# Gating mix with tokens on partitions, in products of 512 columns, turned back by DMA

## The chip, the core and the metric

The kernel runs on one core of one Trainium2 chip. The metric is the device time of one execution in microseconds: 1327.77 us before, the median of 3 runs (1327.48 to 1327.86). The engines are named as in the profile: PE is TensorE (PEld its weight load), DVE is VectorE, ACT is ScalarE, POOL is GpSimd, SP is SyncE, which here issues nearly all DMAs.

## What is computed

Two layers of a trunk. In each, one projection of the normalised input feeds four branches (A gated position mixing, B pooling, C latent attention, D stick-breaking attention), which are gated, summed and projected back. The change touches branch A only:

```python
def spatial_gating(u, v, ln_g, ln_b, w_s, b_s):
    b, s, _ = v.shape
    v = layer_norm(v, ln_g, ln_b)
    nb = s // SGU_BLOCK                                        # 4 blocks of 128 tokens
    vb = v.reshape(b, nb, SGU_BLOCK, SGU_GROUPS, SGU_GROUP_DIM)  # 4 groups of 128 channels
    pos_chunk = jnp.arange(SGU_BLOCK) // CHUNK
    mask = pos_chunk[None, :] <= pos_chunk[:, None]
    w = jnp.where(mask[None], w_s, jnp.zeros_like(w_s))
    mixed = jnp.einsum('gts,bnsgc->bntgc', w, vb) + b_s.T[None, None, :, :, None]
    return u * mixed.reshape(b, s, SGU_WIDTH)
```

Sequence 512, model width 1024, gating width 512.

## The kernel before

Every engine runs a program written out by hand, with semaphores between them. Values are float32; a product is made of three, since each operand is split into a high and a low part (`mm3`, lines 597 to 599: high x high, high x low, low x high). 128x128 blocks of weights are the stationary operand and up to 512 columns of activations the moving one, or the other way round.

**The weights** come in chunks of 8 blocks, in the order of `ORDER` (`chunk_order`), through a ring of four slots. For a chunk, SP loads `w_raw` once the chunk four before it is done (L464), ACT writes the rounded high part `w_hi` (L1037, where `weights_up_to` stands in ACT's program), and POOL subtracts to get `w_lo` (two instructions, L570 and L572). PE waits for `w_lo` before it starts the chunk.

**The stretch around the change**, in PE's order: the projection `bz2`; `mix`; the projection `bz3`; `kq0` (keys, then queries, of heads 0 and 1 into banks 0 to 3); then the first `pair_c` (p = 0): gates `gb0` to `gb3`, products of branch B `yb0`, `yb1`, the scores of two heads, `cz0`, `cz1`, the attention output of head 0 ("att0"), then the second `pair_c` (p = 1), which begins with `kq1`, the output of head 1 ("att1") and `gb4`.

- On PE, `mix` has for each of 4 groups and 4 token blocks one `mm3` of 128 columns: stationary the normalised values (`vn_hi`, `vn_lo`), moving the mixing weights. The result has channels on partitions, which is how it is needed. Then `pe.wait_ge(off_made)` and `bz3`.
- On ACT, `bz(2, 6)` (L1176) waits for the end of `bz2`, and `weights_up_to(l, "kq0")` behind it makes `w_hi` of `bz3`.
- On DVE, `front` makes `mix_off` (per channel and position: the bias and the norm's shift), then `gate_z(2)`, `gate_p(2)`, `b_low(2)`, `rope_tables()`, and then the four instructions of L1735, which take the four banks out of PSUM, scale by channel and add `mix_off` into `mix_t`. They release `mix_taken`, for which PE waits before the queries of `kq0`. `keys_summed` comes next.
- `mix_t` is read late, by `heads_d` (L1950).
- In `pair_c` on ACT, L1298 (`weights_up_to(l, kq, 7)`) is followed by the exponentials of head 0, which wait for the scores' maxima on DVE.
- In `pair_c` on DVE, near the end: `merge_p(0)`, `keys_low(n, 0)`, `gate_c(n, 6)`, `merge_p(1)`, `gate_c(n + 1, 7)`, `keys_low(n + 1, 1)`, `out_gated(n, 6)`, `out_low(n)`. `merge_p` (L1786) joins the two-byte halves of probabilities that a DMA has turned. ACT's `keys_high(n + 1, 1)` (L1239) waits for the second `merge_p(1)` copy; behind it on ACT stand `w_hi` of `gb4`, `keys_squared(l, 1)` with a load of a function table, and `out_high(n)`; DVE's `out_low(n)` follows, and PE's `gb4` waits for that (`act_c_made`).
- Turning by DMA is in use already for keys, queries and probabilities: ACT copies a float32 tile into two planes of two-byte halves (L1256, L1233), SP issues a `DMA_TRANSPOSE` (L471, L485), and DVE or ACT joins the halves again (L1861, L1786).

Of the kernel before, what the change touches and what calls it, by code (L numbers as in the profile page):

```python
# [7 lines left out]
F32 = mybir.dt.float32  # L8
# [8 lines left out]
P = 128  # L17
# [3 lines left out]
G = 4  # L21
# [108 lines left out]
def build(nc, x_in, p_in, pos_in, w_in, par_in, rows_in, const_in, out):  # L130
    ctx = ExitStack()
    with ctx:
# [40 lines left out]
        def plan(start, stop, *items):  # L173
# [22 lines left out]
        vn_hi, vn_lo, rows, mix_off, ln_t = plan(  # L196
            36, 58, ("vn_hi", [TB, SEQ], F32R), ("vn_lo", [TB, SEQ], F32R), ("rows", [SEQ], F32),
            ("mix_off", [G, P], F32), ("ln_t", [P], F32))
# [17 lines left out]
        (mix_t,) = plan(16, 24, ("mix_t", [G, SEQ], F32))  # L216
        k_tok, k_rot, q_tok = plan(36, 46, ("k_tok", [PAIR, TB, P], F32), ("k_rot", [TB, PAIR, 2, HALF], F32),
# [19 lines left out]
        (k_swap,) = plan(13, 14, ("k_swap", [TB, 2, HALF], F32))  # L237
# [35 lines left out]
        def sems(names):  # L273
# [18 lines left out]
        lat_squared, lat_var, lat_root, lat_scaled, lat_taken, lat_halved, lat_hi_made, lat_made = sems(  # L292
            "lat_squared lat_var lat_root lat_scaled lat_taken lat_halved lat_hi_made lat_made")
# [5 lines left out]
        mix_ready, mix_taken, krr_made = sems("mix_ready mix_taken krr_made")  # L299
# [157 lines left out]
        def _(sync):  # L457
# [22 lines left out]

            def turn_p(n, h):
# [35 lines left out]
            for l in range(DEPTH):  # L517
                for name in ORDER:
# [11 lines left out]
                    if name == "bx2":  # L530
                        turn_lat(l)
                    if name in TURNS_C:
                        p, h = TURNS_C[name]
                        turn_p(l * G + PAIR * p + h, h)
# [53 lines left out]
        def _(pe):  # L588
# [108 lines left out]
            def front(l):  # L697
# [45 lines left out]
                for g in range(G):  # L743
                    if g < 2:
                        pe.wait_ge(pooled, after(l * G + 3 - g))
                    for t in range(TB):
                        last = mm3(ps[:, g * 512 + t * P:g * 512 + (t + 1) * P], vn_hi[:, t, g * P:(g + 1) * P],
                                   vn_lo[:, t, g * P:(g + 1) * P], w_hi[:, g, :], w_lo[:, g, :])
# [279 lines left out]
        def _(act):  # L1028
# [222 lines left out]
            def pair_c(l, p):  # L1251
# [46 lines left out]
                weights_up_to(l, kq, 7)  # L1298
                exponentials(n, 0)
# [177 lines left out]
        def _(dve):  # L1477
# [80 lines left out]
            def front(l):  # L1558
# [161 lines left out]
                for g in range(G):  # L1720
                    c = slice(g * P, (g + 1) * P)
                    last = dve.scalar_tensor_tensor(mix_off[:, g, :], bank(5)[:, c], sm("ln_col", G + g), rows[:, c],
# [6 lines left out]
                rope_tables()  # L1729
                for g in range(G):  # L1730
                    if g < G - 1:
                        dve.wait_ge(mix_ready, after(l * (G - 1) + g))
                    else:
                        dve.wait_ge(*end_of(l, "mix"))
                    dve.scalar_tensor_tensor(mix_t[:, g, :].rearrange("p (t s) -> p t s", t=TB),  # L1735
                                             bank(g).rearrange("p (t s) -> p t s", t=TB), sm("ln_col", g),
                                             over(mix_off[:, g, :], [P, TB, P], 1), ALU.mult, ALU.add).then_inc(
# [435 lines left out]
```

## Time and profile before

| | |
|---|---|
| median of 3 runs | 1327.77 us |
| profiled execution | 1328.13 us, its span 1326.3 us |
| PE busy | 1319.2 us, 99% of the span |
| PEld, DVE, ACT, POOL busy | 83%, 58%, 49%, 47% |
| granted TensorE clock | 1.00 throughout |
| chain that ended last | PE 93%, DVE 4% |
| DMA engines' mean share | 38.6% for the busiest queue |

The span runs from the first to the last instruction; 1.8 us of the profiled execution lie around it. A matmul's duration in the trace covers its pipeline; what it costs in a stream is the distance between two starts. In a timeline the columns are start, duration, engine, line, operation, operands and count, then in brackets the idle time of the engine before it and what ended it.

### The profile page before, as it was taken

How to read it: one execution, taken by the hardware profiler on the slowest of the kernel's cores; microseconds unless marked ns; L12 is line 12 of the kernel's file. 1: busy time of each engine (PE TensorE's matmuls, PEld its weight loads, DVE VectorE, ACT ScalarE, POOL GpSimd, SP SyncE). 2: the span in 40 equal slices, each digit the busy share in tenths (PEclk: the TensorE clock that was granted, in tenths of full speed). 3: DMA queues.
4: the chain of work that ended last, by engine and by line, in shares of the span. 5: the costliest groups of instructions: out<-in, count | busy, mean ns of one | idle time of the engine just before them, and what ended most of it. 6: DMA issues, size and time to landing. Idle time of an engine off the chain costs nothing.

```text
span 1326.3 us, 15805 instructions
## 1 busy us (share of the span) xinstructions
PE 1319.2 (99%) x6103; PEld 1106.0 (83%) x6103; DVE 767.8 (58%) x1133; ACT 651.4 (49%) x979; POOL 621.3 (47%) x455
## 2 busy tenths in 40 slices
PE   9999999999999999999999999999999999999998
PEld 8778888888888888888888888888888888888887
DVE  7998676166663223274779976662666533333743
ACT  6478686266652222224455586754666422222242
POOL 2445353454444444455464543444444544444552
PEclk9999999999999999999999999999999999999999
DMA  7425554343343322323344264452433433333332
GB/s 213 117 78 127 128 148 105 94 115 99 100 115 96 95 95 96 112 95 96 97 119 119 87 143 106 125 123 92 107 108 103 112 95 96 96 97 117 101 97 95
DMA packets 141930, 144.63 MB, mean 109 GB/s; under 512 B 82704, under 2 KB 111648, under 8 KB 141856
## 3 DMA queue, kind: packets, MB, share of 16 engines
q1 hardware_dynamic: 140624, 143.08, 38.6%
q8 instruction: 48, 0.79, 0.3%
q10 hardware_dynamic: 1232, 0.55, 0.2%
q14 instruction: 26, 0.21, 0.1%
HBM read 123.15 MB, written 2.10 MB: 94 GB/s over the span
## 4 chain that ended last, share of the span: by engine, by line
PE 93%; DVE 4%; SPq 1%; ACT 1%; DMA 0%; issue 0%; ACTq 0%
PE ps L597 31%; PE ps L599 31%; PE ps L598 31%; SPq L464 1%; PE ps L784 1%; DVE n_t L1605 0%; DVE h_lo L1487 0%; DVE trail_a L1637 0%; DVE pool_lo L1487 0%; DVE trail_b L1637 0%; DVE xb L1640 0%; DVE vn_lo L1487 0%; DVE r_b L1595 0%; DMA par<-par_in 0%; DMA w_raw<-w_in 0%
## 5 line engine op out<-in xcount | busy, mean ns | idle before, releaser
L570 POOL TENSOR_TENSOR w_lo<-w_raw,w_hi 128x512 fp32r<-128x512 f32 x222 | 312.4, 1407 | 680.3 <-ACT w_hi L1037 680.0
L597 PE MATMUL ps<-h_hi,w_hi 128*128 128x512 f32 x1152 | 449.3, 390 | 1.8 <-DVE h_lo L1487 1.8
L599 PE MATMUL ps<-h_hi,w_lo 128*128 128x512 f32 x1152 | 448.4, 389 | 0.0
L598 PE MATMUL ps<-h_lo,w_hi 128*128 128x512 f32 x1152 | 448.4, 389 | 0.0
L1037 ACT ACTIVATE w_hi<-w_raw 128x1024 fp32r<-128x1024 f32 x227 | 238.4, 1051 | 160.6 <-PE ps L599 154.9
L572 POOL TENSOR_TENSOR w_lo<-w_raw,w_hi 128x512 fp32r<-128x512 f32 x222 | 312.0, 1405 | 0.0
L597 PEld LDWEIGHTS ps<-h_hi,w_hi 128*128 128x128 f32 x1152 | 216.2, 188 | 48.1 <-DVE h_lo L1487 3.4
L599 PEld LDWEIGHTS ps<-h_hi,w_lo 128*128 128x128 f32 x1152 | 216.2, 188 | 45.2
L598 PEld LDWEIGHTS ps<-h_lo,w_hi 128*128 128x128 f32 x1152 | 216.3, 188 | 44.3
L1976 DVE SCALAR_TENSOR_TENSOR m_part<-th,ps 128x512 f32<-128x512 f32 x48 | 33.0, 688 | 237.8 <-PE ps L599 237.7
L1336 ACT ACTIVATE th<-ps 128x512 f32<-128x512 f32 x48 | 28.7, 597 | 182.0 <-PE ps L599 182.0
L597 PE MATMUL ps<-act_hi,w_hi 128*128 128x512 f32 x192 | 74.8, 390 | 0.0
L598 PE MATMUL ps<-act_lo,w_hi 128*128 128x512 f32 x192 | 74.7, 389 | 0.0
L599 PE MATMUL ps<-act_hi,w_lo 128*128 128x512 f32 x192 | 74.7, 389 | 0.0
L597 PE MATMUL ps<-m_hi,w_hi 128*128 128x512 f32 x128 | 49.8, 389 | 0.0
L598 PE MATMUL ps<-m_lo,w_hi 128*128 128x512 f32 x128 | 49.8, 389 | 0.0
L599 PE MATMUL ps<-m_hi,w_lo 128*128 128x512 f32 x128 | 49.8, 389 | 0.0
L599 PEld LDWEIGHTS ps<-act_hi,w_lo 128*128 128x128 f32 x192 | 36.0, 188 | 7.5
L598 PEld LDWEIGHTS ps<-act_lo,w_hi 128*128 128x128 f32 x192 | 36.0, 188 | 7.4
L597 PEld LDWEIGHTS ps<-act_hi,w_hi 128*128 128x128 f32 x192 | 36.0, 188 | 7.4
L1427 ACT ACTIVATE o_sq<-x 128x512 f32<-128x512 f32 x16 | 10.1, 634 | 63.8 <-DVE x L2005 63.8
L597 PE MATMUL ps<-w_hi,act_hi 128*128 128x512 f32 (+1 forms) x96 | 36.9, 384 | 0.0
(341 smaller groups left out, 2098.7 us busy)
## 6 DMA issues: line engine op xcount, KB each, us to landing
w_raw<-w_in SPq DMA_DIRECT2D x180, 512.0 KB, 3.5
w_raw<-w_in SPq DMA_DIRECT2D x92, 128.0 KB, 2.5
w_raw<-w_in SPq DMA_DIRECT2D x36, 256.0 KB, 3.1
x<-x_in SPq DMA_DIRECT2D x8, 256.0 KB, 4.6
w_raw<-w_in SPq DMA_DIRECT2D x32, 64.0 KB, 2.1
out_x<-x SPq DMA_DIRECT2D x7, 256.0 KB, 4.0
p_raw<-p_in SPq DMA_DIRECT2D x2, 512.0 KB, 4.6
w_raw<-w_in ACTq DMA_DIRECT2D x4, 128.0 KB, 3.0
```

What stands on the lines that cost most here:

```text
L464: sync.dma_start(to, part).then_inc(raw_loaded[c % RING], 16)
L570: pool.tensor_tensor(w_lo_t[s][:, 0:4, :], w_raw_t[s][:, 0:4, :], w_hi_t[s][:, 0:4, :].bitcast(F32), ALU.subtract)
L572: pool.tensor_tensor(w_lo_t[s][:, 4:8, :], w_raw_t[s][:, 4:8, :], w_hi_t[s][:, 4:8, :].bitcast(F32), ALU.subtract).then_inc(w_lo_made, 1)
L597: pe.matmul(o, a_hi, b_hi, start=first, stop=False, skip_group_check=skip)
L598: pe.matmul(o, a_hi, b_lo, start=False, stop=False, skip_group_check=skip)
L599: return pe.matmul(o, a_lo, b_hi, start=False, stop=last, skip_group_check=skip)
L784: last = pe.matmul(ps[:, s:s + keys], q[at_, b * P:keys], k[at_, 0:keys], start=False, stop=q is qr_lo, skip_group_check=True)
L1037: act.activation(w_hi_t[s][:, 0:n, :], w_raw_t[s][:, 0:n, :], ACT.Copy).then_inc(w_hi_made, 1)
L1336: act.activation(th[:, i % 4, :], bank(b), ACT.Tanh, scale=0.5).then_inc(g_tanh, 1)
L1427: act.activation(o_sq[:, d % 2, :], tile(x, d), ACT.Square).then_inc(o_squared, 1)
L1976: dve.scalar_tensor_tensor(o, th[:, i % 4, :], 1.0, bank(b), ALU.add, ALU.mult).then_inc(y_taken, 1)
```

## The change

The mixing weights become stationary and the normalised values moving: one `mm3` for each group, 512 columns (four runs of 128 that stand 512 apart), so 12 products in place of 48 in each layer. The result has tokens on partitions. DVE copies the four banks as they are into `mix_tok`, now ahead of `rope_tables()`. In `pair_c` with p = 0, ACT splits each group into two-byte halves (`mix_half`), SP turns it (4 `DMA_TRANSPOSE`, ahead of those of `kq1`), and DVE joins the halves in `mix_t` behind `gate_c(n, 6)`, scales and shifts groups 0 and 1 there and groups 2 and 3 in `pair_c` with p = 1. `mix_off` and `k_swap` have other places. The semaphores `landed[6]` and `landed[7]` count the new transfers too.

```diff
@@ sync, new; called ahead of TURNS_C when name == "kq1" @@
+            def turn_mix(l):
+                for g in range(G):
+                    sync.wait_ge(mix_halved, after(l * G + g))
+                    sync.dma_start_transpose(mix_turned[:, g, :].bitcast(U16).rearrange("p (j s) -> p j s", s=P),
+                                             mix_half[:, g, :].bitcast(U16)).then_inc(landed[6 + g % 2], 16)
@@ tensor, front @@
-                    for t in range(TB):
-                        last = mm3(ps[:, g * 512 + t * P:g * 512 + (t + 1) * P], vn_hi[:, t, g * P:(g + 1) * P],
-                                   vn_lo[:, t, g * P:(g + 1) * P], w_hi[:, g, :], w_lo[:, g, :])
+                    c = slice(g * P, (g + 1) * P)
+                    last = mm3(bank(g).rearrange("p (t c) -> p t c", t=TB), w_hi[:, g, :], w_lo[:, g, :], vn_hi[:, :, c],
+                               vn_lo[:, :, c])
@@ scalar, pair_c @@
                 weights_up_to(l, kq, 7)
+                if p == 0:
+                    for g in range(G):
+                        act.wait_ge(mix_taken, after(l * G + g))
+                        act.activation(plane_tiles(mix_half[:, g, :], 0, SEQ), by_tile(mix_tok[:, g, :], 0, SEQ),
+                                       ACT.Copy).then_inc(mix_halved, 1)
                 exponentials(n, 0)
@@ vector, front @@
                 b_low(2)
-                rope_tables()
                 for g in range(G):
                     ...
-                    dve.scalar_tensor_tensor(mix_t[:, g, :].rearrange("p (t s) -> p t s", t=TB),
-                                             bank(g).rearrange("p (t s) -> p t s", t=TB), sm("ln_col", g),
-                                             over(mix_off[:, g, :], [P, TB, P], 1), ALU.mult, ALU.add).then_inc(
-                                                 mix_taken, 1)
+                    dve.tensor_copy(mix_tok[:, g, :], bank(g)).then_inc(mix_taken, 1)
+                rope_tables()
                 keys_summed(l, 0)
@@ vector, new @@
+            def mix_merged(l, g):
+                dve.wait_ge(landed[6 + g % 2], 16 + 16 * after(l * (G + 2) + g // 2))
+                dve.tensor_copy(by_tile(mix_t[:, g, :], 0, SEQ), plane_tiles(mix_turned[:, g, :], 0, SEQ)).then_inc(
+                    dve_step, 1)
+                return step.next()
+            def mix_shifted(l, groups):
+                for g in groups:
+                    by_block = mix_t[:, g, :].rearrange("p (t s) -> p t s", t=TB)
+                    dve.scalar_tensor_tensor(by_block, by_block, sm("ln_col", g),
+                                             over(mix_off[g // 2][:, g % 2, :], [P, TB, P], 1), ALU.mult, ALU.add)
@@ vector, pair_c @@
                 branch_b(l, d + 3, 7)
+                if p:
+                    mix_shifted(l, (2, 3))
                 merge_p(0, lp)
                 keys_low(n, 0)
                 gate_c(n, 6)
+                if p == 0:
+                    for g in range(G):
+                        at_ = mix_merged(l, g)
+                    dve.wait_ge(dve_step, at_)
+                    mix_shifted(l, (0, 1))
                 merge_p(1, lp)
```

## Rows read from the trace of the kernel before

**Rows 1.** The page, part 1: busy time, share of the span, instructions.
```profile
span 1326.3 us, 15805 instructions
PE 1319.2 (99%) x6103; PEld 1106.0 (83%) x6103; DVE 767.8 (58%) x1133; ACT 651.4 (49%) x979; POOL 621.3 (47%) x455
```
**Rows 2.** Waits of PE, the largest: total us, times, longest.
```profile
PE ps L597 <- DVE h_lo L1487: 1.8, 3, 1.0
```
**Rows 3.** Timeline of PE around mix, layer 1.
```profile
96.66 0.39 PE L597 MATMUL ps<-h_hi,w_hi 128*128 128x512 f32 x1
...
97.80 0.22 PE L597 MATMUL ps<-w_hi,vn_hi 128*128 128x128 f32 x1
...
103.11 0.45 PE L597 MATMUL ps<-h_hi,w_hi 128*128 128x512 f32 x1
```
**Rows 4.** Timeline of PE, start of bz3 in layer 2.
```profile
758.73 0.45 PE L597 MATMUL ps<-h_hi,w_hi 128*128 128x512 f32 x1
```
**Rows 5.** Timelines of ACT and POOL ahead of bz3, layer 1; POOL's, layer 2.
```profile
97.54 0.60 ACT L1151 ACTIVATE sz_b<-ps 128x512 f32<-128x512 f32 x1 [0.92 <-PE ps L599]
...
100.40 1.28 POOL L572 TENSOR_TENSOR w_lo<-w_raw,w_hi 128x512 fp32r<-128x512 f32 x1
...
756.03 1.29 POOL L572 TENSOR_TENSOR w_lo<-w_raw,w_hi 128x512 fp32r<-128x512 f32 x1
```
**Rows 6.** Timeline of DVE behind the rope tables, layer 1; ACT's wait for gb1.
```profile
108.75 2.73 DVE L1735 SCALAR_TENSOR_TENSOR mix_t<-ps,small,mix_off 128x512 f32<-128x512 f32 x4
111.41 1.22 DVE L1814 TENSOR_REDUCE small<-k_sq 128x8 f32<-128x1024 f32 x1
...
128.10 0.60 ACT L1216 ACTIVATE th_b<-ps 128x512 f32<-128x512 f32 x1 [1.29 <-PE ps L599]
```
**Rows 7.** Timeline of ACT: a split into halves; the first exponential of head 0.
```profile
119.80 1.12 ACT L1256 ACTIVATE kr_half<-k_rot 128x1024 uint16<-128x1024 uint16 x1
...
144.79 0.78 ACT L1225 ACTIVATE prob<-ps,small 128x512 f32<-128x512 f32 x1 [6.46 <-DVE small L1768]
```
**Rows 8.** Timelines of DVE and POOL where the joins and shifts are put.
```profile
159.72 0.68 DVE L1798 SCALAR_TENSOR_TENSOR sz_c<-sz_c,ps 128x512 f32<-128x512 f32 x1
163.12 0.76 DVE L1786 COPY prob<-p_turned 128x1024 uint16<-128x1024 uint16 x1 [2.73 <-DMA p_turned<-p_half]
164.47 1.05 DVE L1786 COPY prob<-p_turned 128x1536 uint16<-128x1536 uint16 x1 [0.59 <-DMA p_turned<-p_half]
...
160.59 1.29 POOL L570 TENSOR_TENSOR w_lo<-w_raw,w_hi 128x512 fp32r<-128x512 f32 x1 [8.16 <-ACT w_hi L1037]
161.84 1.29 POOL L572 TENSOR_TENSOR w_lo<-w_raw,w_hi 128x512 fp32r<-128x512 f32 x1
```
**Rows 9.** A join of halves that begins while POOL works.
```profile
181.99 1.53 DVE L1861 COPY k_tok<-k_turned 128x1024 uint16<-128x1024 uint16 x1 [1.12 <-DMA k_turned<-k_half]
...
181.61 1.29 POOL L570 TENSOR_TENSOR w_lo<-w_raw,w_hi 128x512 fp32r<-128x512 f32 x1 [3.89 <-ACT w_hi L1037]
```
**Rows 10.** Timelines behind merge_p(1), layer 1: ACT, DVE, then PE's att1 and gb4.
```profile
165.56 1.55 ACT L1239 ACTIVATE pt_hi<-prob 128x512 fp32r<-128x512 f32 x4 [0.79 <-DVE prob L1786]
...
170.44 0.58 ACT L1249 ACTIVATE act_hi<-ps 128x512 fp32r<-128x512 f32 x1
...
171.06 0.69 DVE L1487 TENSOR_TENSOR act_lo<-ps,act_hi 128x512 fp32r<-128x512 f32 x1 [2.53 <-ACT act_hi L1249]
...
171.48 0.39 PE L597 MATMUL ps<-pt_hi,act_hi 128*128 128x512 f32 x1
...
173.34 0.45 PE L597 MATMUL ps<-h_hi,w_hi 128*128 128x512 f32 x1
```
**Rows 11.** The same in layer 2: act_lo of head 0, and gb4.
```profile
826.61 0.69 DVE L1487 TENSOR_TENSOR act_lo<-ps,act_hi 128x512 fp32r<-128x512 f32 x1 [2.53 <-ACT act_hi L1249]
...
828.96 0.45 PE L597 MATMUL ps<-h_hi,w_hi 128*128 128x512 f32 x1
```
**Rows 12.** Timelines of POOL and PE at the chunk dv0, layer 1.
```profile
220.86 1.77 POOL L572 TENSOR_TENSOR w_lo<-w_raw,w_hi 128x512 fp32r<-128x512 f32 x1
...
224.95 0.44 PE L597 MATMUL ps<-w_hi,h_hi 128*128 128x512 f32 x1
```

More of the change, by code:

```diff
@@ L195, in build @@
             ("ckvn_lo", [SEQ], F32R))
-        vn_hi, vn_lo, rows, mix_off, ln_t = plan(
-            36, 58, ("vn_hi", [TB, SEQ], F32R), ("vn_lo", [TB, SEQ], F32R), ("rows", [SEQ], F32),
-            ("mix_off", [G, P], F32), ("ln_t", [P], F32))
+        vn_hi, vn_lo, rows, ln_t = plan(
+            36, 58, ("vn_hi", [TB, SEQ], F32R), ("vn_lo", [TB, SEQ], F32R), ("rows", [SEQ], F32), ("ln_t", [P], F32))
+        mix_off = plan(72, 73, ("mix_off0", [2, P], F32)) + plan(84, 85, ("mix_off1", [2, P], F32))
         lat_t, krs, r_b, n_t, xh = plan(
@@ L216, in build @@
         (mix_t,) = plan(16, 24, ("mix_t", [G, SEQ], F32))
+        (mix_half,) = plan(16, 24, ("mix_half", [G, SEQ], F32))
+        (mix_tok,) = plan(8, 16, ("mix_tok", [G, SEQ], F32))
+        (mix_turned,) = plan(8, 16, ("mix_turned", [G, SEQ], F32))
         k_tok, k_rot, q_tok = plan(36, 46, ("k_tok", [PAIR, TB, P], F32), ("k_rot", [TB, PAIR, 2, HALF], F32),
@@ L236, in build @@
         (q_swap,) = plan(81, 83, ("q_swap", [TB, PAIR, 2, HALF], F32))
-        (k_swap,) = plan(13, 14, ("k_swap", [TB, 2, HALF], F32))
+        (k_swap,) = plan(71, 72, ("k_swap", [TB, 2, HALF], F32))
         d_hi, d_lo = plan(24, 40, ("d_hi", [WIDE], F32R), ("d_lo", [WIDE], F32R))
@@ L291, in build @@
             "gain_diag gain_ready gain_taken h_scaled h_hi_made h_made")
-        lat_squared, lat_var, lat_root, lat_scaled, lat_taken, lat_halved, lat_hi_made, lat_made = sems(
-            "lat_squared lat_var lat_root lat_scaled lat_taken lat_halved lat_hi_made lat_made")
+        lat_squared, lat_var, lat_root, lat_taken, lat_halved, lat_hi_made, lat_made = sems(
+            "lat_squared lat_var lat_root lat_taken lat_halved lat_hi_made lat_made")
         ln_var, ln_root, ln_taken, vn_hi_made, ln_made, wsum_ready, off_made = sems(
@@ L298, in build @@
             "pool_hi_made pool_made p_ready pooled bz_tanh b_made b_hi_made act_b_made")
-        mix_ready, mix_taken, krr_made = sems("mix_ready mix_taken krr_made")
+        mix_ready, mix_taken, mix_halved, krr_made = sems("mix_ready mix_taken mix_halved krr_made")
         k_ready, k_squared, k_var, k_root, k_made, q_squared, q_taken, q_var, q_root, q_rotated = sems(
@@ L531, in _ @@
                         turn_lat(l)
+                    if name == "kq1":
+                        turn_mix(l)
                     if name in TURNS_C:
@@ L1721, in front @@
                     c = slice(g * P, (g + 1) * P)
-                    last = dve.scalar_tensor_tensor(mix_off[:, g, :], bank(5)[:, c], sm("ln_col", G + g), rows[:, c],
+                    last = dve.scalar_tensor_tensor(mix_off[g // 2][:, g % 2, :], bank(5)[:, c], sm("ln_col", G + g), rows[:, c],
                                                     ALU.mult, ALU.add)
@@ L1907, in merge_weights @@
                 a, b = PARTS[u]
-                dve.wait_ge(landed[6 + u], 16 + 16 * after(n))
+                dve.wait_ge(landed[6 + u], 16 + 16 * after(n + 2 * (n // G + 1)))
                 dve.tensor_copy(by_tile(sp, a, b), plane_tiles(s_turned, a, b)).then_inc(a_merged, 1)
```

## The prediction

> **What bounds the kernel now.** I read the page's part 1 first. TensorE (PE) is busy for 1319.2 of 1326.3 us [rows 1], so it is the bound of nearly every stage. PE's list of waits comes next: its largest entry is 1.8 us in three pieces [rows 2]. A change can therefore gain only by taking time out of PE's stream, and it loses wherever it makes PE wait. So the third view is PE's timeline, for the distance between starts. A product of 128 columns costs (103.11 - 97.80) / 48 = 0.111 us, one of 512 costs (97.80 - 96.66) / 5 = 0.228 us [rows 3]: a fourth of the columns for half the price. The fourth is the margin at each chunk and each hand-over behind the change: when the thing PE needs was ready, and when PE took it.
>
> All times below are in the clock of the trace of before. Nearly every engine waits for PE within a few us, so when PE is early all of them move with it; what counts is the margin against PE.
>
> **PE's products.** Per layer 48 x 0.111 = 5.31 us go and 12 x 0.228 = 2.73 us come: 2.58 us less. The new moving operand is read in four runs of 128 columns. No row bounds such a read in this place; I take 0.228 us. It doesn't matter, since a wait follows.
>
> **The wait for bz3.** With 2.73 us PE reaches `bz3` at 97.80 + 2.73 = 100.53. Its `w_lo` is done at 100.40 + 1.28 = 101.68 [rows 5]. This doesn't move with mix: ACT makes `w_hi` of `bz3` behind the tanh of `bz2` at 97.54, whose release is the end of `bz2` on PE, ahead of mix; POOL follows ACT without a pause. With 0.07 us for the hand-over PE starts `bz3` at 101.75 and not at 103.11 [rows 3]: gain 1.36 us. Layer 2: 756.03 + 1.29 + 0.07 = 757.39 against 758.73 [rows 4, 5]: 1.34 us. **So of 5.2 us in both layers, 2.7 us reach PE's stream**, and 1.2 us per layer become idle. The products could cost up to 0.33 us each without any effect.
>
> **DVE in the front.** Four copies out of PSUM replace four instructions of 2.73 us together [rows 6]; DVE shows no float32 copy of this kind there, so I bound them by zero and by those 2.73 us and take the upper end, being the same size out of the same banks. Their place ahead of `rope_tables()` releases `mix_taken` earlier, so PE's queries don't wait for it. `keys_summed` (111.41 before) then starts at about 110.3, 0.3 us late against PE in layer 1 and, where the tables have no other wait, about 1 us in layer 2. Behind it `k_made` and ACT's splits may slip by this, but ACT then idles 1.29 us until `gb1` ends [rows 6]: nothing for PE.
>
> **ACT and SP in pair_c, p = 0.** Four splits at up to 1.12 us each [rows 7] are at most 4.5 us. They stand in front of the first exponential, where ACT is idle for 6.46 us [rows 7]: nothing. If that cover were gone, each us would delay exponentials, probabilities and `merge_p`. SP's four transposes go out in the same idle time, ahead of its wait for the probabilities, and end well before these are made; the load of `kq1` stands behind them but waits for `yb1` anyway: nothing.
>
> **DVE in pair_c, p = 0.** Four joins and two shifts are put behind `gate_c(n, 6)`, which ends at 160.40. DVE now idles there until 163.12 and again 0.59 us before 164.47, for the turned probabilities [rows 8]. An undisturbed join is 0.76 us, in a row about 0.65. But POOL makes `w_lo` of `kq1` from 160.59 on, in two instructions of 1.29 us [rows 8]. The trace shows what happens when they meet: POOL began at 181.61 for 1.29 us, so it ended at 182.90; a join of this very shape began at 181.99 and took 1.53, so it ended 0.62 after POOL did [rows 9]. They alternate. The Trainium skill says the same ("SBUF — State Buffer", section "SBUF: two separate sides"): the port pair that VectorE and GpSimd share is an exclusive lock, and the loser is blocked for the whole instruction. The trace agrees (1.53 against 0.76 us).
>
> Step by step: join 1 from 160.32 to 161.08; POOL's first half behind it to about 162.25; join 2 to 162.87; POOL's second half to 164.05; join 3 to 164.67; join 4 to 165.33; two shifts at 0.68 each (as L1735, 2.73 / 4) to 166.80. `merge_p(1)` has then both parts landed and ends at about 166.72 + 0.64 + 1.05 = 168.41, where it ended at 164.47 + 1.05 = 165.52: **2.9 us late**.
>
> **What this delays.** ACT's `pt_hi` began at 165.56, and ACT worked without a pause from there to `act_hi` of head 0 at 170.44; DVE's `act_lo` ended at 171.06 + 0.69 = 171.75; PE began `gb4`, which waits for it, at 173.34 [rows 10]. The margin is 1.59 us, less 0.07. All of this chain slips by 2.9, so `gb4` begins at 171.75 + 2.89 + 0.07 = 174.71: PE waits 1.37 us. In layer 2 the margin is 828.96 - 827.30 = 1.66 [rows 11]; the same slip, there about 2.97, gives 1.38. Earlier on the way is att1, at 171.48 [rows 10]: its `pt_lo` ends at about 170.8, margin 0.7. So **2.75 us are given back**. The bounds of the inserted work: if DVE never met POOL it would end `merge_p(1)` 0.6 us late, inside the margin, price zero; if all six instructions cost 1.75 us each (1.12 + 0.63, blocked), 7 us late, price 5.5 us per layer. I take the alternation, since the nearest row shows exactly these two instructions.
>
> **DVE in pair_c, p = 1.** Two shifts before `merge_p(0)`, about 1.35 us, with POOL idle. ACT's `w_hi` of `dv0` slips by it, and POOL meets `merge_p(1)` again. `w_lo` of `dv0` was ready at 220.86 + 1.77 = 222.63 for 224.95 [rows 12], margin 2.3. I reckon 2.1 us of slip: nothing, but with 0.1 to 0.2 us left it may cost up to 0.5 per layer. The chain of head 1 behind `gb4` likewise keeps some 0.2 us. These two put the weight of my error on the slow side.
>
> **The sum**, on the profiled execution (span 1326.3, 1328.13 with what lies around): 1328.13 - 2.70 + 2.75 = 1328.2 us. That execution stood 0.36 us above the median, so 1327.8 for the median. For the two thin margins I add 0.2: **1328.0 us**.
>
> **A rule weighed.** By these rows the weight load sets the 128-column product and the 512 columns the other. The Trainium skill ("TensorE: Matmul & The Clock Gate", section "Back-to-back issue gap") gives 81 ns and 131 ns per product for 128 and 512 columns. This case's rows show 111 and 228 ns [rows 3], so the measurement decides; by the page's figures PE would save 3.9 - 1.6 = 2.3 us per layer, which the wait for `bz3` cuts to the same 1.35.
>
> **The rivals.**
> - *Held, nothing given back.* The wait for `bz3` cuts the gain to 2.7 us, and DVE's work fits. It needs `merge_p(1)` to be late by under 1.5 us, so that at most one join loses time to POOL. For it: DVE has 3.3 us of idle time there. Against it: rows 9. 1327.77 - 2.7 = 1325.1; with one join blocked still about 1325.5.
> - *The whole 5.2 us.* `w_lo` of `bz3` would have to be ready 1.2 us sooner; nothing in the diff moves it. 1322.6.
> - *Slower: the joins cost more than the idle time by far.* One mechanism, at the same place: more of the six instructions lose to POOL, or POOL's own halves are drawn out. From 4.2 us of lateness on, PE's wait at `gb4` passes 2.7 us per layer and the kernel is over 0.2% slower; each further blocked instruction adds about 1.1 us per layer. Against it: POOL has only two instructions there. With four blocked: 1327.8 + 2 x 2.2 = 1332; all six: 1336.
> - *The products are not faster.* If a moving operand in runs cost 0.44 us, as much per column as before, PE's stream would keep its length, and the loss at `gb4` stands alone: 1327.77 + 2.75 = 1330.5. Against it: PE already reads other operands in such runs for att0 and att1.
>
> **How the numbers follow.** Chances: forecast 0.72 (1326.3 to 1329.8), held 0.13, whole gain 0.02, joins dear 0.09, products not faster 0.04. A measurement can tell about 0.2%, 2.7 us, from no change: faster means under 1325.1, slower over 1330.4. Half of "held" lies under that edge: faster 0.08. Slower takes most of the last two, and a little of the forecast: 0.13. Same 0.79. The range reaches into "held" and to the edge of slower: 1325.3 to 1330.2.
>
> **What would show each step.** PE: 24 products of 512 columns on `vn_hi`, 0.228 apart, then a wait of about 1.2 us at L597 for POOL's `w_lo`, twice. A second new wait, 1.4 us at `gb4` for DVE's `act_lo`, twice. ACT's idle time before the exponentials down from 6.46 to about 2.5. DVE: two of the four joins at 1.5 to 1.8 us and no idle time before `merge_p(1)`. I am wrong if PE's list has no wait at `gb4`, if `bz3` starts without one, or if a wait stands at a place that is not named here.

## The result, and the profile after

The changed kernel takes 1330.23 us, the median of 20 runs (1327.82 to 1331.45), the kernel before 1327.68 (20 runs beside them, 1327.32 to 1329.02). The ratio is 1.0015, 95% interval 1.0009 to 1.0021: slower by 2 us by this ratio and by 2.6 by the medians, 0.2% at most. I had predicted 1328.0. The changed kernel's runs also lie further apart, over 3.6 us where before's lie over 1.7, and five of the 20 stand within 1 us of before's median; a trace shows one execution, here one of 1330.53 us. The profiled execution of after has a span of 1328.7 us, 2.4 more than before.

The page, part 1: PE has 3.8 us less to do than in [rows 1], and its span is 2.4 us longer. So 6.2 us of new idle time must stand in PE's stream.

```profile
span 1328.7 us, 15693 instructions
PE 1315.4 (99%) x6031; PEld 1099.2 (83%) x6031; DVE 781.6 (59%) x1149; ACT 658.4 (50%) x987; POOL 625.2 (47%) x455
```

PE's list of waits shows where (total us, times, longest). Against [rows 2] three entries are new or larger: `w_lo` twice (`bz3`), `act_lo` (of its three waits 0.65 and 0.98 are those at `gb4`), and **`qr_lo` twice, 0.92 and 1.58, at the scores of the second pair, a place that the prediction doesn't name**.

```profile
PE ps L609 <- DVE qr_lo L1504: 2.5, 2, 1.6
PE ps L609 <- POOL w_lo L584: 2.3, 2, 1.2
PE ps L609 <- DVE act_lo L1504: 1.8, 3, 1.0
PE ps L609 <- DVE h_lo L1504: 1.3, 3, 0.4
```

**The stretch of mix.** PE's timeline, layer 1 (start, duration, ..., idle time before and what ended it), and POOL's last instruction ahead of it. Between the first two rows lie six products: (98.99 - 97.63) / 6 = 0.227 us each, as in [rows 3]. From the start of mix to `bz3` it is 4.04 us where it was 5.31; in layer 2 the gain is 1.26.

```profile
97.63 0.39 PE L609 MATMUL ps<-vn_hi,w_hi 128*128 128x512 f32 x1
98.99 0.39 PE L609 MATMUL ps<-vn_hi,w_hi 128*128 128x512 f32 x1
101.67 0.47 PE L609 MATMUL ps<-h_hi,w_hi 128*128 128x512 f32 x1 [1.16 <-POOL w_lo L584]
...
100.26 1.26 POOL L584 TENSOR_TENSOR w_lo<-w_raw,w_hi 128x512 fp32r<-128x512 f32 x1
```

**The joins and shifts, layer 1.** Timelines of DVE, POOL, ACT and PE; they answer to [rows 8], [rows 7] and [rows 10]. L1805 is the join, L1813 the shift, L1800 `merge_p(1)`.

```profile
158.84 2.66 DVE L1805 COPY mix_t<-mix_turned 128x1024 uint16<-128x1024 uint16 x4
161.53 3.33 DVE L1813 SCALAR_TENSOR_TENSOR mix_t<-mix_t,small,mix_off 128x512 f32<-128x512 f32 x2
164.78 1.68 DVE L1800 COPY prob<-p_turned 128x1024 uint16<-128x1024 uint16 x2
...
159.90 2.70 POOL L582 TENSOR_TENSOR w_lo<-w_raw,w_hi 128x512 fp32r<-128x512 f32 x1 [8.94 <-ACT w_hi L1049]
162.57 1.74 POOL L584 TENSOR_TENSOR w_lo<-w_raw,w_hi 128x512 fp32r<-128x512 f32 x1
...
143.33 0.78 ACT L1237 ACTIVATE prob<-ps,small 128x512 f32<-128x512 f32 x1 [2.66 <-DVE small L1782]
...
172.73 0.50 PE L609 MATMUL ps<-h_hi,w_hi 128*128 128x512 f32 x1 [0.65 <-DVE act_lo L1504]
```

Here the four joins ran undisturbed (2.66 / 4 = 0.67 us apart) and POOL's first half was drawn out to 2.70 us; then the two shifts took 3.33 us beside POOL's second. `merge_p(1)` ended at 166.46. PE is 1.44 us earlier than before at `bz3`, so against PE it is 166.46 + 1.44 - 165.52 = 2.4 us late. In layer 2 the joins took 4.84 us and the shifts 1.42: other instructions lose, and the sum is 6.3 us where it was 6.0. `merge_p(1)` is there 2.75 us late against PE.

**The scores of the second pair, layer 2.** DVE in after, POOL in after, then DVE in the kernel before. The join of `q_turned` begins 3.5 us later than before, where PE is only 0.5 later at `gb4`. Before, both `kn_lo` were done (845.91) when POOL began its chunk (846.21); now they meet it, and so does `qr_lo`: three subtractions take 1.7 to 1.8 us, not 0.7. `qr_lo` ends at 855.70, and PE, which could have started at 854.27, starts at 855.85. The 3.0 us by which the join is later against PE have two parts: the first transpose of `q_turned` is issued at 841.84, 12.4 us behind the start of `gb4` (before: 839.43, 10.5 behind), and it lands 5.5 us after its issue where it took 4.4.

```profile
847.37 0.76 DVE L1889 COPY q_tok<-q_turned 128x1024 uint16<-128x1024 uint16 x1 [2.11 <-DMA q_turned<-q_half]
848.01 3.48 DVE L1508 SCALAR_TENSOR_TENSOR kn_lo<-k_tok,par,kn_hi 128x512 fp32r<-128x512 f32 x2
853.94 1.76 DVE L1504 TENSOR_TENSOR qr_lo<-q_rot,qr_hi 128x512 fp32r<-128x512 f32 x1
...
847.39 1.84 POOL L582 TENSOR_TENSOR w_lo<-w_raw,w_hi 128x512 fp32r<-128x512 f32 x1 [5.08 <-ACT w_hi L1049]
853.86 1.29 POOL L582 TENSOR_TENSOR w_lo<-w_raw,w_hi 128x512 fp32r<-128x512 f32 x1 [2.92 <-ACT w_hi L1049]
```

```profile
843.85 0.76 DVE L1861 COPY q_tok<-q_turned 128x1024 uint16<-128x1024 uint16 x1 [0.71 <-DMA q_turned<-q_half]
844.50 1.41 DVE L1491 SCALAR_TENSOR_TENSOR kn_lo<-k_tok,par,kn_hi 128x512 fp32r<-128x512 f32 x2
850.73 0.69 DVE L1487 TENSOR_TENSOR qr_lo<-q_rot,qr_hi 128x512 fp32r<-128x512 f32 x1 [0.82 <-ACT qr_hi L1283]
```

**The ledger**, from the starts of PE's pieces in both traces, after minus before: up to mix -0.17; mix -1.27 and -1.26; `gb4` +0.83 and +1.16; the scores of pair 2 +1.16 and +1.81; the rest +0.15. Together +2.41, the difference of the spans. (A new wait costs some 0.2 us more here than in the list of waits, since PE's stream also has to start again.)

### The profile page after: what moved, and what is told of

It reads as the page before. It is cut to its first block, busy times and chain, and to the rows that moved or that the text cites. A ratio compares the mean times of both kernels' runs of the same rounds, so it can differ in the third digit from the quotient of the medians.

```text
span 1328.7 us, 15693 instructions
## 1 busy us (share of the span) xinstructions
PE 1315.4 (99%) x6031; PEld 1099.2 (83%) x6031; DVE 781.6 (59%) x1149; ACT 658.4 (50%) x987; POOL 625.2 (47%) x455
## 4 chain that ended last, share of the span: by engine, by line
PE 85%; DVE 9%; ACT 3%; DMA 1%; issue 1%; POOL 0%; ACTq 0%; SPq 0%
PE ps L609 28%; PE ps L610 28%; PE ps L611 28%; DMA q_turned<-q_half 1%; DVE small L1781 1%; DVE mix_t L1805 1%; ACT w_hi L1049 1%; PE ps L659 1%; PE ps L669 0%; DVE prob L1800 0%; PE ps L796 0%; DVE n_t L1622 0%; DVE kn_lo L1508 0%; PE ps L674 0%; DVE prob L1793 0%
```

## The experiments

Theory T as it stood before the first experiment: bz3's `w_lo` caps the gain, DVE's six instructions ahead of `merge_p(1)` make the loss, at `gb4` and, inherited, at the scores. The rival R puts the loss on the parts that I had costed at nothing: ACT's splits, SP's transposes, the moved copies.

The kernel before ran beside each of them and had medians of 1327.57 to 1327.76, so the times can be compared across experiments. Each has 11 runs (5 where said), and in the traces the start of the first mix varies by up to 0.8 us between kernels that do the same up to there, without a cause that I know: differences of half a us between two medians prove nothing by themselves, and I lean on the places of the waits.

### Without DVE's joins and shifts

```diff
-                if p:
-                    mix_shifted(l, (2, 3))
...
-                        at_ = mix_merged(l, g)
-                    dve.wait_ge(dve_step, at_)
-                    mix_shifted(l, (0, 1))
+                        dve.wait_ge(landed[6 + g % 2], 16 + 16 * after(l * (G + 2) + g // 2))
```

> The changed kernel without DVE's four joins and four shifts in pair_c; everything else of the change stays: the 512-column products, the copies out of PSUM, ACT's four splits, the four transposes, the waits for their landing. Left out: mix_t is never formed, branch A is gated with x in its place, so the time is that of the kernel without the six and two DVE instructions. Theory T (the loss is made by DVE's work ahead of merge_p(1), and by the two shifts of p = 1): no PE wait at gb4, none at the scores of pair 2, the two waits for bz3's w_lo stay at 1.2 us each; total 1325.0 us (before's 1327.7 less 2.7). Rival R (the loss comes from ACT's splits, the transposes' DMA traffic or the moved copies): about 1330, waits at gb4 (0.7, 1.0) and at the scores (0.9, 1.6) unchanged.

Measured: 1326.79 us, ratio to before 0.9992 (0.9983 to 1.0001). PE's waits:

```profile
PE ps L609 <- POOL w_lo L584: 2.3, 2, 1.2
PE ps L609 <- DVE qr_lo L1504: 2.0, 2, 1.5
...
PE ps L609 <- DVE act_lo L1504: 0.2, 1, 0.2
```

The waits at `gb4` are gone, and the time is 3.4 us lower: by the two traces 2.0 of it lie at `gb4`, 0.7 at the scores and 0.65 ahead of the first mix, which is the varying start. **But at the scores 0.51 and 1.46 us stay**: of the 2.5 us only 0.5 hang on DVE's work. T is right for `gb4` and wrong for the scores.

### The shifts behind merge_p(1) and gate_c

```diff
-                    dve.wait_ge(dve_step, at_)
-                    mix_shifted(l, (0, 1))
                 merge_p(1, lp)
                 gate_c(n + 1, 7)
+                if p == 0:
+                    dve.wait_ge(dve_step, at_)
+                    settle(mix_shifted(l, (0, 1)))
                 keys_low(n + 1, 1)
```

> The changed kernel with the two shifts of groups 0 and 1 (3.4 us in the trace of after, stretched by POOL) moved behind merge_p(1) and gate_c(n+1, 7); the joins stay where they are. T: merge_p(1) is late by some 0 to 1 us and not by 2.3, so gb4 waits for nothing or up to 0.3 us, and the scores of pair 2, whose lateness I hold to be inherited, wait less: 1325 to 1326.5. R: 1330, as after. A third case: the shifts delay keys_low(n+1, 1) and out_gated, and the wait at gb4 comes back from there: 1328 to 1330.

Measured: 1329.73 us, 1.0017 (1.0008 to 1.0026), 0.5 below after, which is no clear difference. `gb4` waits no more, but att1 does, for `pt_lo` (first line, PE's waits): behind the shifts the four subtractions of `keys_low` run into POOL and take 3.88 us for 1.70 (second line, DVE).

```profile
PE ps L609 <- DVE pt_lo L1504: 2.1, 2, 1.2
...
166.70 3.88 DVE L1504 TENSOR_TENSOR pt_lo<-prob,pt_hi 128x512 fp32r<-128x512 f32 x4
```

The third case had the mechanism; the place was att1. So moving the shifts only moved their cost. T had 1325 to 1326.5 here and fell.

### w_hi of bz3 first

```diff
                 b_high(1)
+                weights_up_to(l, "bz3")
                 bz(2, 6)
                 weights_up_to(l, "kq0")
```

> The changed kernel with w_hi of bz3 made by ACT ahead of its work behind bz2 instead of behind it, so that POOL can make w_lo before PE ends mix. T: the two waits of 1.2 us at bz3 vanish, all behind moves with PE, the margins at gb4 and at the scores are against PE, but the chain behind merge_p(1) also moves as it hangs on PE: 1330.2 - 2.3 = 1327.9. Rival: the chain behind bz3 doesn't move with PE and the 2.3 us come back as longer waits at gb4: 1330.2.

Measured: 1327.26 us, 0.9994 (0.9986 to 1.0003), 3.0 below after; by the traces 2.5 of it lie between the start of mix and `bz3`. `bz3` starts without a wait in both layers, and what follows moves with PE: `gb4` waits 0.73 and 0.96, the scores 1.10 and 1.59, as in after within 0.2. This confirms the cap on the gain, and that margins are rightly counted against PE.

### The kernel before, with six such DVE instructions

```diff
                 gate_c(n, 6)
+                if p == 0:
+                    for g in range(G):
+                        dve.tensor_copy(by_tile(merged[:, 4 + g, :], 0, SEQ), plane_tiles(mix_t[:, g, :], 0, SEQ)).then_inc(
+                            dve_step, 1)
+                        at_ = step.next()
+                    dve.wait_ge(dve_step, at_)
+                    for g in range(2):
+                        by_block = merged[:, 4 + g, :].rearrange("p (t s) -> p t s", t=TB)
+                        dve.scalar_tensor_tensor(by_block, mix_t[:, g, :].rearrange("p (t s) -> p t s", t=TB), sm("ln_col", g),
+                                                 over(ones[:], [P, TB, P], 1), ALU.mult, ALU.add)
                 merge_p(1, lp)
```

> The kernel before, with six DVE instructions of the same shapes put in the same place of pair_c, p = 0, between gate_c(n, 6) and merge_p(1): four joins of two-byte halves (of mix_t into tiles of merged that are written later anyway) and two scaled additions. Nothing else of the change. T: merge_p(1) is late by 2.3 to 3 us, PE waits at gb4 for 0.7 to 1.4 us and at the scores of pair 2 for 0.9 to 1.6 us, in both layers: 1331 to 1333. The prediction's one-place version: gb4 alone, +2.75, 1330.4. R (other parts make the loss): 1327.7, no new PE wait.

Measured: 1330.08 us, 1.0016 (1.0008 to 1.0025): +2.3. PE waits at `gb4` for 0.98 and 0.95, and not at all at the scores (the entry `qr_lo` is missing from its list). It is the prediction's one-place version, 2.75 expected; T's own 1331 to 1333 fell. So DVE's work alone makes a loss at `gb4`, 1.1 us per layer, and no wait at the scores. It does make the pieces there late: in layer 2 `q_turned` is issued 12.1 us behind the start of `gb4`, not 10.5, and joined 16.1 behind it, not 14.9. That lateness alone costs PE nothing, so the 3 us at the scores need a second cause.

### What stands at the scores: PE's own program

In after and in all three variants of it above the first transpose of `q_turned` in layer 2 lands 5.4 to 5.5 us after its issue, in the kernel before and in the one with six instructions after 4.4 and 4.0. Two answers on the DMA engines, after (841 to 846 us) and before (839 to 843.6; queue: packets, MB, share of 16 engines; then KB and median us from issue to landing). After has two lines more, q8 and q14, both "instruction".

```profile
q1 hardware_dynamic: 1784, 0.90, 119.9%
q8 instruction: 1, 0.02, 1.8%
q14 instruction: 1, 0.01, 0.4%
...
q_turned<-q_half SPq DMA_TRANSPOSE x2, 5.3
```

```profile
q1 hardware_dynamic: 2303, 1.02, 106.2%
...
q_turned<-q_half SPq DMA_TRANSPOSE x2, 4.2
```

Queue 8 brings 16384 bytes 48 times in an execution, 786432 bytes in all, and PE's compiled program has 786816. I take it for PE's program, fetched while it runs: in the two kernels below whose program of PE is longer than before's, the queue brings 49 such pieces. The change took 144 instructions of 64 bytes out of it (796032 bytes before), so each fetch came at another place of the work. In after it began at 844.43 us and took 1.46 (the median is 1.03), and by the trace's DMA records 32 data packets start between 845.25 and 846.5, where 180 to 280 per quarter of a us are usual in the transposes. Before, it came at 827.42, ahead of the transposes. Theory F: this fetch holds up the transposes, and the lateness runs DVE into POOL. The next kernels leave the data flow as it is and move only PE's fetches, all of them at once. Queue 14 is not the cause: it also brings a piece amid these transposes in the kernel whose length is restored, at 842.98, where there is no delay, and none in the kernel before made longer, where there is one.

**144 idle waits at the start of after.**

```diff
                     pe.matmul(ps[:, 7 * 512:7 * 512 + P], ones[:], ones[:], start=True, stop=True)
+                for _ in range(144):
+                    pe.wait_ge(ones_made, after(0))
```

> The changed kernel with 144 waits on a semaphore that has long been set, put in PE's program behind the first products that wake the clock. The change took 144 instructions out of PE's program (12430 records to 12286), and with that each fetch of 16384 bytes of PE's program (48 of them in either kernel) comes at another place of the work: in layer 2 at 844.43 us, during the transposes of q_turned, where the kernel before had it at 827.42. Theory F (this fetch holds up the transposes): with the 144 instructions back the fetch of layer 2 falls again before the keys, q_turned lands 4.0 to 4.4 us after its issue and not 5.5, and PE's wait at the scores of pair 2 in layer 2 (1.5 us) is gone or under 0.5; gb4's waits (0.7, 1.0) and bz3's (1.2 twice) stay. Time 1330.2 - 1.5 plus what 144 waits cost at the start, 0 to 4 us, which is read from where lat0 begins. Rival D (the delay comes from DVE's work or from the other changes of the queues): the 5.5 us and the wait of 1.5 stay.

Measured: 1334.81 us (5 runs). The first projection begins 5.0 us later than in after (11.71 against 6.75), and by bx3, the projection at 53 us, PE is 6.5 us late. It has fallen 7.1 us behind by 17 us and makes up 0.6 of it. The 2.1 us beyond 5.0 stand where the clock was low: PE had no product from 7.2 to 11.7 us and was granted half of its clock (0.50, the 1.2 GHz level) from 10 to 16 us, where after has 1.00 throughout. The row gives the stretch, what each engine did in it, then the granted clock, the DMA share and GB/s.

```profile
10.00:16.00 6.00, 4.29 (x12) 3.84 (x13) 5.67 (x8) 5.75 (x10) 0.00 (x0) 0.50 1.05 326
```

Without the 6.5 us the time is 1328.3, 1.9 below after. A wait by itself takes 32 bytes of the program, not 64, so the fetch moved by half of what I wanted, to 841.96, 5.6 us ahead of the issue of `q_turned`. That was enough: `q_turned` lands after 4.03 us, and **the waits at the scores are zero in both layers**, with `bz3` (1.15 twice) and `gb4` (0.65, 0.99) as they were. R and D fall for the scores: every part of the change is still there.

**112 of them in the kernel before** put the fetch at 827.07, not where I meant it, for the same reason: `q_turned` 4.28 us, no wait, 1332.05 us (5 runs) with 3.9 lost ahead of the first mix. It tests nothing of F's forecast, though it agrees with it.

```diff
+                for _ in range(112):
+                    pe.wait_ge(ones_made, after(0))
```

> The kernel before with 112 such waits at the same place, 256 - 144, so that in layer 2 the fetches fall where they fall in the changed kernel. F: q_turned of layer 2 lands 5.5 us after its issue and not 4.4; its margin at the scores of pair 2 was 2.1 us, so PE waits there for 0 to 1.5 us; nothing else changes but the start (0 to 3 us). D: 4.4 us, no wait.

```diff
                 pe.matmul(o, a_hi, b_hi, start=first, stop=False, skip_group_check=skip)
+                rest()
                 pe.matmul(o, a_hi, b_lo, start=False, stop=False, skip_group_check=skip)
+                rest()
...
+            def rest():
+                if spread[0]:
+                    spread[0] -= 1
+                    pe.wait_ge(ones_made, after(0))
+                    pe.wait_ge(consts_made, after(0))
...
                 norm_total(l)
+                if l == 0:
+                    spread[0] = 144
```

> The changed kernel with waits on semaphores that have long been set between the products of the first projections of layer 0, 144 places, so that PE's program is as long as that of the kernel before (796032 bytes; the changed kernel's has 786816, and the 144 waits at the start gave 791424). F (the fetch of PE's program holds up the transposes): the fetches fall again as in the kernel before, in layer 1 near 173 us, ahead of the keys' transposes, and in layer 2 near 826, q_turned lands after 4.0 to 4.4 us, and the waits at the scores of pair 2 (0.9 and 1.6) are gone or under 0.5; gb4's (0.7, 1.0) and bz3's (1.2 twice) stay. A wait between two products is to cost nothing, since PE works on the product before: 1327.5 to 1328.5. If each cost 34 ns as in the row of waits at the start, 4.9 us come on top: 1332.5. D: the waits at the scores stay, 1330 or more.

Measured: **1327.63 us**, 1.0000 (0.9992 to 1.0009), 2.6 below after, by an edit that computes nothing. The fetch of layer 2 is at 829.34 (that of layer 1 at 167.03, not near 173 as expected, since in layer 1 only half of the removed instructions are missing yet and all 144 pairs have passed), `q_turned` takes 3.9 us, and the list has no `qr_lo`; `gb4` still waits 0.99 and 0.96 (PE's waits; a new one of 1.2 us, for `mask_d`, is the first pair waiting for its semaphore, and bx3's falls from 1.26 to 0.37):

```profile
PE ps L617 <- POOL w_lo L584: 2.3, 2, 1.2
PE ps L617 <- DVE act_lo L1516: 2.1, 3, 1.0
PE ps L619 <- DVE mask_d L1547: 1.2, 1, 1.2
```

**The converse: the fetches alone, in the kernel before.** 112 pairs make its program 803200 bytes, 16384 longer than that of after.

```diff
+                if l == 0:
+                    spread[0] = 112
```

> The kernel before with 112 pairs of free waits between the products of layer 0's first projections, which make PE's program 7168 bytes longer (803200), so that in layer 2 its fetches come at the places of the work where the changed kernel has them. Nothing of the change itself is in it. F: the fetch of layer 2 is at 14 to 16 us behind the start of gb4, during the transposes of q_turned; these land 5.3 to 5.6 us after issue instead of 4.4, three of DVE's subtractions meet POOL, and PE waits at the scores of pair 2 for 0.3 to 1.6 us in layer 2; in layer 1, where the fetches now fall some 14 us behind gb4 too, perhaps as well: 1328.0 to 1330.5 against 1327.8. D (the rest of the change is needed for the delay): 4.4 us, no wait, 1327.8.

Measured: 1328.79 us, 1.0010 (1.0001 to 1.0019), 1.2 slower than before. The fetch of layer 2 is at 843.33, 15.1 us behind the start of `gb4` as in after (15.0). PE's wait, the DMA rows (839 to 844 us) and DVE's: at the scores the same picture as in after, with nothing of the change in the kernel.

```profile
PE ps L605 <- DVE qr_lo L1499: 1.2, 1, 1.2
...
q8 instruction: 1, 0.02, 1.4%
...
q_turned<-q_half SPq DMA_TRANSPOSE x2, 5.4
...
846.26 3.49 DVE L1503 SCALAR_TENSOR_TENSOR kn_lo<-k_tok,par,kn_hi 128x512 fp32r<-128x512 f32 x2
852.19 1.76 DVE L1499 TENSOR_TENSOR qr_lo<-q_rot,qr_hi 128x512 fp32r<-128x512 f32 x1
```

In layer 1 the fetch was at 188.43, behind the transposes (`q_turned` 4.44), and there was no wait; that "perhaps" was a miss.

| layer 2 | program of PE, bytes | fetch behind start of gb4 | q_turned issued behind start of gb4 | issue to landing | join behind start of gb4 | wait at the scores |
|---|---|---|---|---|---|---|
| before | 796032 | -1.5 | 10.5 | 4.40 | 14.9 | 0 |
| before with six DVE instructions | 796032 | 0.6 | 12.1 | 3.99 | 16.1 | 0 |
| after | 786816 | 15.0 | 12.4 | 5.50 | 17.9 | 1.58 |
| after, no DVE work | 786816 | 15.5 | 12.2 | 5.52 | 17.7 | 1.46 |
| after, 144 at the start | 791424 | 7.1 | 12.7 | 4.03 | 16.7 | 0 |
| after, length restored | 796032 | 0.4 | 12.4 | 3.91 | 16.3 | 0 |
| before, 7168 longer | 803200 | 15.1 | 11.7 | 5.70 | 17.4 | 1.18 |

In layer 2 no kernel waits whose join begins up to 16.7 us behind the start of `gb4` (six kernels), and all wait, 1.2 to 1.6 us, where it begins 17.4 or more behind (eight). It takes two delays to get there, a late issue and a late landing. In after the late issue is there with or without the fetch (12.4 in both), and the fetch adds the late landing. In the longer kernel before and in the one without DVE's work a fetch makes the late issue too: an earlier one, at 817.31 and 815.53, falls on the last transposes of the probabilities, which land 5.9 and 6.1 us after their issue and not 4.7, so that `merge_p(1)` and all behind it are 1.2 and 1.4 us late against `gb4`. In after that fetch (817.70, 6.2 us) costs nothing more, since DVE is still at its shifts when they land. No run has the late landing alone.

### Where DVE's work can stand

**Fourth join and shifts behind out_gated.**

```diff
+        mix_off0 = sb("mix_off0", [P, 2, P])
...
-                    for g in range(G):
-                        at_ = mix_merged(l, g)
-                    dve.wait_ge(dve_step, at_)
-                    mix_shifted(l, (0, 1))
+                    for g in range(3):
+                        mix_merged(l, g)
...
                 out_gated(n, 6)
+                if p == 0:
+                    dve.wait_ge(dve_step, mix_merged(l, 3))
+                    mix_shifted(l, (0, 1))
```

> The changed kernel, where the fourth join and the shifts of groups 0 and 1 stand behind out_gated(n, 6), in the 2.5 us in which DVE waits for ACT's act_hi; mix_off0 has a place of its own for that. Three joins stay ahead of merge_p(1). If the shifts and the fourth join make merge_p(1) late: it ends with less than 1 us of delay, no wait at gb4 and none at att1, and DVE's work costs nothing more than in the kernel that leaves it out: 1326.8 to 1327.5, with bz3's two waits and the 1.5 us at the scores of layer 2 left. If instead act_lo slips (2.1 us of work in 2.5 us of idle time, with POOL working beside it), gb4 waits for 0.3 to 1 us again: 1328 to 1329.5.

Measured: 1329.09 us, 1.0011 (1.0002 to 1.0020), the second case. DVE and POOL: 2.1 us of work took 3.9 in the 2.53 us of idle time, since POOL makes a chunk there, and `act_lo` began 1.3 us after its `act_hi` was done; `gb4` waits 0.55 and 0.82.

```profile
168.19 1.60 DVE L1806 COPY mix_t<-mix_turned 128x1024 uint16<-128x1024 uint16 x1
169.82 2.29 DVE L1814 SCALAR_TENSOR_TENSOR mix_t<-mix_t,small,mix_off 128x512 f32<-128x512 f32 x2
...
167.89 1.29 POOL L583 TENSOR_TENSOR w_lo<-w_raw,w_hi 128x512 fp32r<-128x512 f32 x1 [4.48 <-ACT w_hi L1050]
169.13 1.77 POOL L585 TENSOR_TENSOR w_lo<-w_raw,w_hi 128x512 fp32r<-128x512 f32 x1
```

The same with bz3's weights first:

```diff
+                weights_up_to(l, "bz3")
                 bz(2, 6)
```

> The same, and w_hi of bz3 made ahead of ACT's work behind bz2 (it took 2.97 us off the changed kernel by itself). The two should add up: 1324.0 to 1325.0, which beats the kernel before by 0.2 to 0.3%. If part of it is given back at gb4 or at the scores of pair 2: 1326 to 1327.

Measured: 1327.34 us, 0.9997 (0.9988 to 1.0006): 0.3 above the second case, with 0.24 and 0.93 at `gb4`, 1.05 and 1.58 at the scores.

**All shifts in p = 1, ahead of the maxima.** The two calls of `mix_shifted` in the changed kernel go, and `mix_off0` has its own place again:

```diff
                 branch_b(l, d + 2, 7)
+                if p:
+                    dve.wait_ge(dve_step, step.n)
+                    mix_shifted(l, (0, 1, 2, 3))
                 maxima(n, 0)
```

> The changed kernel with all four shifts in pair_c of p = 1, ahead of the maxima of its first head, where DVE idled for 4 us in the first pair (mix_off0 has a place of its own for that); the four joins stay. If the shifts, stretched by POOL, are what makes merge_p(1) late: it is late by less than 0.5 us, gb4 doesn't wait, and the time falls by 1.6 us to 1328.5, with bz3's waits and those at the scores (0.5 to 0.9 and 1.5) left. If the joins alone make it late, gb4 still waits for 0.5 or more in layer 2: 1329.5 to 1330.

Measured: 1328.05 us, 1.0001 (0.9992 to 1.0010), 2.2 below after. No wait at `gb4`, and bz3's stay, as expected; the scores' are 1.10 and 1.20, where I expected 0.5 to 0.9 and 1.5. The joins alone fit into DVE's idle time: behind them it waits again, 1.55 us, for the turned probabilities.

```profile
158.19 2.65 DVE L1806 COPY mix_t<-mix_turned 128x1024 uint16<-128x1024 uint16 x4
162.39 2.39 DVE L1801 COPY prob<-p_turned 128x1024 uint16<-128x1024 uint16 x2 [1.55 <-DMA p_turned<-p_half]
```

### All three

The diffs of the weights first, the length restored and the shifts in p = 1, in one kernel:

```diff
+                weights_up_to(l, "bz3")
...
+                    spread[0] = 144
...
+                    mix_shifted(l, (0, 1, 2, 3))
```

> All three: shifts in p = 1, w_hi of bz3 ahead of ACT's work behind bz2, and PE's program as long as before. If the three causes are all there is, the products' whole gain of 5.2 us is kept: 1322.5 to 1323.5, ratio to the kernel before 0.996 to 0.997. If something further gives it back, PE shows a wait at a place not yet named, 1325 or more.

Measured: **1322.81 us** (5 runs, 1322.41 to 1322.99), 0.9962 (0.9949 to 0.9976): 5.0 us below the kernel before and 7.4 below after. The three edits alone gave 3.0, 2.6 and 2.2, in sum 7.8. PE's list has no wait for `w_lo`, `act_lo` at `gb4`, or `qr_lo` left:

```profile
PE ps L618 <- DVE h_lo L1518: 1.2, 3, 0.4
PE ps L711 <- DVE ones L1565: 1.1, 1, 1.1
PE ps L618 <- issue: 0.7, 1, 0.7
PE ps L670 <- DVE w_hi L1569: 0.4, 1, 0.4
PE ps L618 <- DVE act_lo L1518: 0.2, 1, 0.2
...
195.56 4.82 DVE L1827 SCALAR_TENSOR_TENSOR mix_t<-mix_t,small,mix_off 128x512 f32<-128x512 f32 x4
```

The last row is DVE's four shifts: 4.82 us, most of them beside POOL. They fill the 3.98 us in which DVE idled there, waiting for the scores, and make the first maxima 0.75 us later behind the start of the scores (5.70 us against 4.95 before); PE waits for none of it.

## Why the prediction was right, and where it was not

The time came out within the range and "same" was right, but 1330.2 lies at the very end of the range, and partly by luck: one term was missing (+2.97 us), and another was 0.76 us too large and made up for a quarter of it.

- **The products**: 0.227 us measured, 0.228 taken. Right.
- **The wait for bz3**: POOL's `w_lo` was done at 101.52 (forecast 101.68), PE started at 101.67 (101.75), waiting 1.16. Gain 1.27 + 1.26 = 2.53, forecast 2.70. Right, and shown by the early `w_hi`, which gave back 2.5 us at this place.
- **The front on DVE, the splits, the transposes**: `keys_summed` at 110.02 (forecast 110.3); ACT idle for 2.66 us before the exponentials (forecast 2.5); no wait hangs on them. The four splits were 3.88 us, under the 4.5 that I allowed.
- **Joins and shifts ahead of merge_p(1)**: I had them end at 166.80, 6.5 us after their start; they took 6.0 in layer 1 and 6.3 in layer 2. The alternation was right in kind and wrong in detail for layer 1, where DVE kept its turn through four joins. `merge_p(1)` was 2.4 us late in layer 1 and 2.75 in layer 2, not 2.9 and 2.97, and `gb4` cost 0.83 + 1.16 = 1.99, not 2.75. The kernel with six instructions shows this term alone: 2.3. The margins, 1.5 to 1.6 us, were right: with them the measured lateness gives 0.86 and 1.16. That behind `gb4` this lateness costs nothing by itself was right too; but it brought the join of `q_turned` 1.6 and 1.2 us nearer to the scores.
- **dv0**: no wait. The 0.2 us for thin margins were not needed there.
- **The step that failed** is how the waits were looked for. The prediction takes "the margin at each chunk and each hand-over behind the change" from the data flow alone and has no term for the scores. I counted the products as time only. They are also instructions, and taking 144 of them away moved the fetches of PE's program against the work. That cost 1.16 + 1.81 = 2.97 us at the scores, together with DVE's work, without which 0.5 us less is lost there; restoring the length gave back 2.6. The trace of before shows queue 8 in the answer on the DMA engines (48 packets), and I hadn't looked at what it carries. The closing sentence, that a wait at an unnamed place would prove me wrong, applies.

With the measured terms the sum is 1328.13 - 0.17 - 2.53 + 1.99 + 2.97 + 0.15 = 1330.5; the profiled execution of after took 1330.53, as it must, since the ledger leaves nothing out.

Of the rivals, "slower" had the right direction and the wrong place: all it says happens at `gb4`, and there the cost was below the forecast.

What stays open: in layer 1 the fetch falls at 178 to 180 us, on the first transpose of `k_turned`, whose issue by SP then took 1.84 to 2.16 us in all seven kernels with that program length and 1.23 in the others. Again DVE's work alone is too little: with it and without the fetch `q_turned` is joined 16.2 to 16.5 us behind the start of `gb4`, and PE doesn't wait (three kernels); with both it is 17.1 to 17.5, and PE waits 0.9 to 1.1 (five). At 16.6 it waits 0.51 in one kernel (no DVE work) and not at all in another (shifts behind `gate_c`), which I can't explain. Nor did I show by which path one fetch stops all transposes; that it does is shown. And the wider spread of the changed kernel's times, which a fetch that falls now on the transposes and now beside them would explain, is in no trace.

## What to carry to other kernels

When PE bounds a kernel, ask of a faster stage first what PE will wait for next: here the weights for the following chunk, and the cure was one line on ACT. Put work for DVE where POOL is idle or where nothing waits for DVE's next result; the shifts cost 2.2 us ahead of `merge_p(1)`, nearly as much behind it, and no wait of PE ahead of the maxima. And when a change in the number of instructions leaves a difference of 1 to 3 us at a place that it doesn't touch, look at the instruction queues and shift the program's length by free waits before you look for a cause in the data flow. Put these waits between products, in pairs: in one row on an idle PE they cost 5.0 us and then 1.5 more, behind a fall of the clock.

## What the runs showed of the hardware

- PE's program comes in fetches of 16384 bytes while it runs, 48 of them for 786816 to 796032 bytes and 49 for 799616 and 803200. Where one fell amid the transposes of `q_turned` in layer 2, the first of these landed after 5.3 to 5.7 us (eight kernels, one of them without the change), elsewhere after 3.8 to 4.4 (six kernels); in each of the eight another fetch fell on the last transposes of the probabilities, which landed after 5.9 to 6.2 us and not after 4.6 to 4.9. The Trainium skill ("Runtime: NRT & Kernel Launch", section "Instruction fetch mechanics") says that crossing a block of 16 KiB costs one tail increment, mostly hidden. The size agrees; the cost doesn't in this case, where one fetch falls amid transposes that PE will wait for: moving the fetches gave 2.6 us of device time, 0.2%.
- A row of waits of PE on semaphores long set put off its next product by 5.0 us for 144 and 3.4 us for 112, 34 and 31 ns each, where PE had nothing else to do. Pairs of them between products of 512 columns cost nothing: these stayed 0.23 us apart.
- In the kernel with 144 waits at the start PE had no product from 7.2 to 11.7 us, and its granted clock fell from 1.00 to 0.50 near 10 us and stayed there until some 16 us; four products of 448 columns took 1.83 us in it, not 1.06.
- DVE and POOL: in layer 1 POOL's subtraction was held for 2.70 us while DVE ran four joins back to back, in layer 2 they took turns. The rule weighed in the prediction, an exclusive lock by the Trainium skill's "SBUF — State Buffer", section "SBUF: two separate sides", fits both; who gets the next turn does not follow from it.
